# Two buffers instead of four for the rotation tables of a state-space mixer, rebuilt between the rotations

## The chip, the cores and the metric

One core of a Trainium2 chip runs the whole program, in float32. The metric is the device time of one execution in microseconds (us), the median of several. Five engines work side by side, each through its own instruction stream in order, and wait for one another on semaphores: PE (TensorE, matrix products), DVE (VectorE), ACT (ScalarE), POOL (GpSimd) and SP (here only the queue of DMA issues).

## What is computed

256 tokens of width 1024 go through three layers: a windowed-attention layer with a dense feed-forward, a forgetting-attention layer with 8 experts, and a hybrid layer (three mixers side by side) with 32 small experts. The change lies in one of the mixers of the third layer, a diagonal complex recurrence over 2048 states:

```python
mag = jnp.exp(a_re * dt)
lam_re = mag * jnp.cos(a_im * dt)
lam_im = mag * jnp.sin(a_im * dt)
...
bu_re = jnp.einsum('blgh,gph->blgp', ug, bb_re)
bu_im = jnp.einsum('blgh,gph->blgp', ug, bb_im)
_, _, h_re, h_im = lax.associative_scan(_complex_affine_combine, (lr, li, bu_re, bu_im), axis=1)
y = (jnp.einsum('blgp,ghp->blgh', h_re, c_re.astype(f32))
     - jnp.einsum('blgp,ghp->blgh', h_im, c_im.astype(f32)))
```

The output of the whole program is the normalised x after the third layer, 256 by 1024.

## The kernel before, in words

The 2048 states lie as 16 steps of 128 partitions by 256 tokens. The kernel turns the input of each state by the angle of its own decay, so that the recurrence becomes two real ones with the factor `mag`, which DVE can scan, and turns the result back. For this it needs cos and sin of 1 to 256 times the angle. They lie in four tables of 2048 columns, table q for the steps 4q to 4q+3; `s5_table(q)` says where. POOL builds a table by doubling, in `table(q, at)`: eight steps, of n = 1, 2, 4, up to 128 columns for each of four states, each of six instructions, and every one of them waits for POOL's own last result. `at` is a scratch place.

The work on step i, with q = i // 4:

- PE (`s5_steps`, the matmul helper on L704) writes two 128x256 products into the bank PB[6]; before that it waits until DVE has read those of step i-1. A step of PE later than i = 4q+4 also computes the output of the four steps of q (L1123), once POOL has turned them back.
- DVE (`turn_and_scan`, L1907 on) waits at the first step of each q for table q, then multiplies the products by the table (its helper is on L1482) and scans them (L1929, L1931).
- POOL (`turned_back`, L2720 on) waits for the scan of step i and for the output of q-1 and turns back, in six instructions (L2728 to L2735). I call this rotation i.

Where the tables lie: table 0 in GB (otherwise the gains of the norms), table 1 in the arena, table 2 at the arena's end, table 3 in Y. Y is free only after the norm "n3", which ends the expert layer. So POOL builds tables 0 to 2 early, beside the experts of the second layer (about 660 to 727 us), then does its half of the norm, builds table 3, and after that does the 16 rotations.

PE's and DVE's other work is woven in between the steps, by generators (`second_block`, `along`, `weave`): first z tiles (PE, L1140), then projections (L1093, L1102) with the first part of a recurrent mixer (`rw_first`; DVE L2010 to L2032, PE L1166), then an attention over eight heads (PE L830 scores, L842 to L846 transposes, L861 and L862; DVE L1604 mask, L1612 maxima, L1631 and L1632 normalising). The order is fixed when the program is written: an engine that waits at one step holds up all that stands behind it in its stream. In DVE's stream, step 8 stands ahead of L2019, and step 12 ahead of the mask of the third head and the normalising of the second.

The weights come by DMA into ring slots, each issued by SP when the chunk before it in the slot has been read.

Of the kernel before, what the change touches and what calls it, by code (L numbers as in the profile page):

```python
# [176 lines left out]
def drive(g):  # L177
    for _ in g:
        pass
# [22 lines left out]
def along(main, side, nm, ns):  # L202

    for k, _ in enumerate(main):
        if k % nm == nm - 1:
            for _ in range(ns):
                next(side, None)
# [23 lines left out]
def build(nc, dr, out, dbg=None):  # L231
    ctx = ExitStack()
    with ctx:
        dbg = dbg or {}

        def sb(name, n, dt=F32):
            return ctx.enter_context(nc.sbuf_tensor(name, [128, n], dt))
# [11 lines left out]
        XT = sb("XT", 8 * T)  # L249
        Y = sb("Y", 2 * D)  # L250
        GB = sb("GB", 2 * D)
        AR = sb("arena", 24080)
        SM = sb("small", 1024)
        IX = sb("ix", 64, U32)
        POS = sb("pos", T, I32)
# [9 lines left out]

        def ar(at, *shape):
            n = int(np.prod(shape))
            assert at + n <= 24080, (at, n)
            a = AR[:, at:at + n]
            if len(shape) == 2:  # L270
                return a.rearrange("p (a b) -> p a b", a=shape[0])
            if len(shape) == 3:
                return a.rearrange("p (a b c) -> p a b c", a=shape[0], b=shape[1])
            return a

        F = lambda a: a.rearrange("p a b -> p (a b)")
# [31 lines left out]
        GT = ar(3072, EARLY, 3, T)  # L308
        zT = ar(6144, 14 * 257).rearrange("p (i t) -> p i t", i=14)
        W0 = 6144 + 14 * 257  # L310
        S0 = W0 + 9728
        LW = ar(S0 + 1280, 2, 512)
        E0 = W0 + 5632
        BBt, CTt = ar(E0, 2, 512), ar(E0 + 1024, 2, 512)
        GN3 = ar(S0 + 512, 2048)
        Z = ar(10496, 2, 512)
        b5, c5 = ar(11520, 512), ar(12032, 512)
        w1, w2 = ar(12544, 16, 16), ar(12800, 16, 16)
# [24 lines left out]
        s_cum, s_ncum, s_rw1, s_rw2, s_lora, s_b5, s_c5, s_out = [  # L343
            sem("s_" + n) for n in ("cum", "ncum", "router1", "router2", "lora", "s5b", "s5c", "out")]
# [38 lines left out]
        lnM, lnP, lnD = sig("ln_gain", NORMS), sig("ln_row0", NORMS), sig("ln_row1", NORMS)  # L383
# [31 lines left out]
        tbG = sig("s5_table", range(4))  # L415
# [141 lines left out]
        for h in range(12):  # L557
            b, g = 64 * (h % 2), h // 4
# [3 lines left out]
                            v=[Vn[:, 0, g * 64:g * 64 + 64], Vn[:, 1, g * 64:g * 64 + 64]], out=mixT[:, h // 2, :]))  # L562
# [73 lines left out]

        def s5_table(q):

            t = (GB[:, :], ar(E0 + 2048, 2048), ar(S0 + 2560, 2048), Y[:, :])[q]
            return t.rearrange("p (x k t) -> p x k t", x=2, k=4)  # L640

        s5_m, s5_g = ar(S0, 2, T), ar(S0 + 512, T)
# [832 lines left out]
        def vector_program(v):  # L1475
# [111 lines left out]
            def attention(l):  # L1587
                hs, (S, PT, stat) = heads[l], abuf(l)
                n, ob = len(hs), out_banks[l]
                for i in range(n + 3):  # L1590
                    if i < n:
                        h, b = hs[i], i % 2
                        w0 = width(h)
                        wd = w0 + 256
                        sb_, st = S[i % 3], stat[:, i % 16, :]
                        v.wait_ge(*scP.at((l, i)))
                        src = PB[b]
                        if h["kind"] != "mem":
                            if i >= 3:
                                v.wait_ge(*ptP.at((l, i - 3)))  # L1600
                            if (l, i) == (2, 0):
                                v.wait_ge(*tbG.at(3))
                            if h["kind"] == "moba":
                                ins = v.scalar_tensor_tensor(sb_[:, 0:wd], c["dist"], h["slope"], src[:, 0:wd], ALU.mult, ALU.add)  # L1604
                            else:
                                ins = tt_(sb_[:, 0:wd], src[:, 0:wd], c["swa"] if h["kind"] == "swa" else c["caus"], ALU.add)
                            ins.then_inc(*DV.up(mkD, (l, i)))
                            v.wait_ge(*DV.last)
                            src = sb_
                        sink = "sink" in h  # L1610
                        v.tensor_reduce(st[:, 0:1], src[:, 0:w0], AX.X, ALU.max, negate=True).then_inc(*DV.up())
                        ins = v.tensor_reduce(st[:, 1:2], src[:, w0:wd], AX.X, ALU.max, negate=True)  # L1612
                        if sink:
                            ins.then_inc(*DV.up())
                            v.wait_ge(*DV.last)
                            v.tensor_scalar(st[:, 0:2], st[:, 0:2], nsink[:, h["sink"]:h["sink"] + 1], None, ALU.min).then_inc(*DV.up())
                            v.wait_ge(*DV.last)
                            ins = v.tensor_scalar(st[:, 4:6], st[:, 0:2], v_["sink"][:, h["sink"]:h["sink"] + 1], None, ALU.add)
                        ins.then_inc(*DV.up(mxD, (l, i)))
# [553 lines left out]
            n = 0  # L2173
# [100 lines left out]
        def scalar_program(a):  # L2274
# [197 lines left out]
            norm("n3")  # L2472
            a.wait_ge(*lnP.at("n3"))
            a.wait_ge(*lnD.at("n3"))
            a.dma_start(F(LW), dr["lora"]).then_inc(s_lora, 16)


            turned("x4")
# [202 lines left out]
        def gpsimd_program(g):  # L2681
# [57 lines left out]
            g.wait_ge(*scD_.at("cos"))  # L2739
            g.wait_ge(*scA_.at("sin"))  # L2740
            g.wait_ge(*lnD.at("n2"))
            for q in range(3):
                drive(table(q, S0))
            norm("n3")
            g.wait_ge(*lnP.at("n3"))
            g.wait_ge(*lnD.at("n3"))
            drive(table(3, W0 + 3072))
            for q in range(4):
                drive(turned_back(q))
            for st in ("n4", "n5"):  # L2750
                norm(st)

# [213 lines left out]
```

## Time and profile before

| | |
|---|---|
| three runs | 2149.57 us median, 2147.04 to 2153.64 |
| the profiled execution | 2149.57 us, span 2147.8 us |
| PE busy | 1940.7 us (90%) |
| DVE, ACT, POOL busy | 517.6, 255.9, 170.0 us |
| mean granted clock of PE | 0.956 |

The span is the time from the first to the last instruction; 1.8 us lie around it. The rows below are read like this: a start in us from the span's beginning, a duration, the engine, the line, the operation, what it writes and reads, and in brackets how long the engine had been idle before it and what ended that. The granted clock is 1.00 at PE's upper level of 2.4 GHz and 0.50 at the lower, 1.2 GHz.

The stage of the change lies between 1411 and 1608 us. In the rows `pb` is PSUM, `arena`, `GB`, `Y`, `X`, `XT`, `ringbuf` and `small` are buffers in SBUF, `cst` and `vec` constants.

### The profile page before, as it was taken

The numbers are of one execution on the slowest core, as the hardware profiler recorded it, in microseconds if no ns is written. First come the engines' busy times: TensorE is split into PE (matmuls) and PEld (weight loads), VectorE is DVE, ScalarE is ACT, GpSimd is POOL, SyncE is SP. The second block draws the span as 40 slices with busy tenths as digits, with TensorE's granted clock in tenths as the row PEclk, the third lists the DMA queues.
The fourth block names the chain that finished last, engine by engine and source line by source line (L and its number), as shares of the span: only waits on it lengthen the run. The fifth ranks groups of instructions, "written<-read, shape, count | busy, mean of one in ns | idle before, by whom it ended". The sixth has DMA issues, their size and how long they took to land.

```text
span 2147.8 us, 47628 instructions
## 1 busy us (share of the span) xinstructions
PE 1940.7 (90%) x22158; PEld 1529.0 (71%) x22158; DVE 517.6 (24%) x1204; ACT 255.9 (12%) x630; POOL 170.0 (8%) x309
## 2 busy tenths in 40 slices
PE   7998999899899999999999999977789999968764
PEld 6756885467489899999989898855457778643321
DVE  1632000222311101011100101135574332132223
ACT  1211000022111000000000000021132111010001
POOL 0000000100006400000000000054340000000000
PEclk9998999899879999999999999988899999979998
DMA  7233433321358989899898989740111045549995
GB/s 281 88 118 137 151 145 126 147 99 58 139 206 334 384 340 373 354 346 370 327 389 325 380 330 385 270 160 4 75 64 47 32 166 237 208 175 428 427 427 227
DMA packets 41009, 498.20 MB, mean 232 GB/s; under 512 B 5448, under 2 KB 5984, under 8 KB 7264
## 3 DMA queue, kind: packets, MB, share of 16 engines
q1 hardware_dynamic: 38992, 493.25, 58.1%
q8 instruction: 178, 2.92, 0.5%
q10 hardware_dynamic: 1808, 1.78, 0.3%
q14 instruction: 31, 0.25, 0.0%
HBM read 493.94 MB, written 1.05 MB: 230 GB/s over the span
## 4 chain that ended last, share of the span: by engine, by line
PE 81%; DVE 7%; DMA 7%; issue 2%; ACT 2%; DVEq 0%; SPq 0%
PE pb L1001 22%; PE pb L1020 11%; PE pb L695 11%; PE pb L704 6%; PE pb L700 5%; DMA ringbuf<-in_e2in 4%; PE pb L768 4%; PE pb L903 4%; DVE arena L1482 2%; PE pb L1152 2%; PE pb L1417 2%; PE pb L944 2%; PE pb L1140 2%; PE pb L830 1%; PE pb L789 1%
## 5 line engine op out<-in xcount | busy, mean ns | idle before, releaser
L1001 PE MATMUL pb<-arena,ringbuf 128*64 128x80 f32 (+1 forms) x9856 | 481.5, 240 | 5.9 <-issue 5.7
L1001 PEld LDWEIGHTS pb<-arena,ringbuf 128*64 128x64 f32 (+1 forms) x9856 | 464.5, 145 | 25.8 <-issue 11.5
L1020 PE MATMUL pb<-arena,ringbuf 128*64 128x80 f32 (+1 forms) x4928 | 232.5, 239 | 6.2 <-issue 6.2
L1020 PEld LDWEIGHTS pb<-arena,ringbuf 128*64 128x64 f32 (+1 forms) x4928 | 228.3, 145 | 10.1 <-issue 7.8
L1482 DVE TENSOR_TENSOR arena<-arena,pb 128x160 f32<-128x160 f32 (+3 forms) x154 | 58.1, 377 | 716.5 <-ACT arena L2459 438.3
L695 PE MATMUL pb<-XT,ringbuf 128*128 128x256 f32 (+1 forms) x976 | 217.9, 385 | 3.0 <-ACT XT L2276 1.9
L695 PEld LDWEIGHTS pb<-XT,ringbuf 128*128 128x128 f32 (+1 forms) x976 | 186.8, 192 | 32.1 <-issue 3.2
L2276 ACT ACTIVATE arena<-pb 128x256 f32<-128x256 f32 (+4 forms) x163 | 68.2, 436 | 474.3 <-PE pb L1020 114.0
L704 PE MATMUL pb<-arena 64*64 64x64 f32 (+4 forms) x664 | 107.5, 325 | 15.4 <-ACT ringbuf L2557 4.4
L704 PEld LDWEIGHTS pb<-arena 64*64 64x64 f32 (+4 forms) x664 | 52.4, 154 | 68.0 <-issue 38.5
L2684 POOL TENSOR_TENSOR X<-Y,GB 128x1024 f32<-128x1024 f32 x5 | 11.7, 2340 | 1106.6 <-DVE Y L1482 1106.6
L2459 ACT ACTIVATE arena<-pb 128x160 f32<-128x160 f32 x88 | 26.8, 304 | 585.4 <-PE pb L1001 585.4
L768 PE MATMUL pb<-XT,ringbuf 128*128 128x256 f32 x400 | 95.2, 390 | 0.9 <-ACT XT L2276 0.9
L700 PE MATMUL pb<-ringbuf,arena 128*128 128x512 f32 x192 | 85.1, 604 | 2.8 <-DVE arena L1482 1.8
L768 PEld LDWEIGHTS pb<-XT,ringbuf 128*128 128x128 f32 x400 | 75.2, 194 | 16.4 <-issue 5.7
L903 PE MATMUL pb<-ringbuf,arena 128*128 128x512 f32 x176 | 75.7, 592 | 0.0
L700 PEld LDWEIGHTS pb<-ringbuf,arena 128*128 128x128 f32 x192 | 37.0, 194 | 49.5 <-issue 47.3
L726 PE MATMUL pb<-cst,X 128*128 128x128 f32 x96 | 23.2, 423 | 51.8 <-POOL X L2684 41.8
L903 PEld LDWEIGHTS pb<-ringbuf,arena 128*128 128x128 f32 x176 | 33.4, 190 | 41.7 <-issue 41.4
L1449 PE MATMUL pb<-ringbuf,arena 128*32 128x512 f32 x272 | 38.7, 693 | 24.2 <-DMA ringbuf<-in_e2in 24.2
L726 PEld LDWEIGHTS pb<-cst,X 128*128 128x128 f32 x96 | 18.9, 223 | 58.3 <-POOL X L2684 45.9
L944 PEld LDWEIGHTS pb<-arena,X 128*64 128x64 f32 (+1 forms) x768 | 52.5, 167 | 10.1 <-DVE arena L1482 4.8
(349 smaller groups left out, 1909.1 us busy)
## 6 DMA issues: line engine op xcount, KB each, us to landing
ringbuf<-in_ein SPq DMA_DIRECT2D x88, 2048.0 KB, 10.3
ringbuf<-in_eout SPq DMA_DIRECT2D x64, 1408.0 KB, 7.6
ringbuf<-in_e2in SPq DMA_DIRECT2D x17, 2048.0 KB, 30.6
arena<-in_e2in SPq DMA_DIRECT2D x15, 2048.0 KB, 27.0
ringbuf<-in_fin SPq DMA_DIRECT2D x11, 2048.0 KB, 7.7
ringbuf<-in_e2out SPq DMA_DIRECT2D x10, 2048.0 KB, 23.3
ringbuf<-in_wo SPq DMA_DIRECT2D x6, 2048.0 KB, 7.9
ringbuf<-in_gate SPq DMA_DIRECT2D x8, 1536.0 KB, 7.5
```

Source lines behind the costliest of these rows:

```text
L695: ins = pe.matmul(outp, w[:, j, col:col + m], rT[:, j, :], start=j == 0, stop=j == kt - 1)
L700: ins = pe.matmul(outp, aT[:, j, tt * 128:(tt + 1) * 128], w[:, j, col:col + n], start=j == 0, stop=j == kt - 1)
L704: return pe.matmul(o, l, r, start=True, stop=True)
L768: ins = pe.matmul(PB[b][:, i * 256:i * 256 + 256], held["p"][:, j, (col0 + i) * 128:(col0 + i + 1) * 128], xT[:, j, :], start=j == 0, stop ...
L903: ins = pe.matmul(PB[2 * h + tt][:, :], hT[:, f + j, tt * 128:(tt + 1) * 128], w3[:, j, h * 512:(h + 1) * 512], start=f + j == 0, stop=f + ...
L944: ins = pe.matmul(PB[b][h_, k * n:(k + 1) * n], x3[:, tt, dt_ * 128 + h_.start:dt_ * 128 + h_.stop], PS_[i][:, tt, :], start=tt == 0, stop ...
L1001: ins = pe.matmul(PB[b][h_, t * C1:(t + 1) * C1], w3[:, k, t * 128 + h_.start:t * 128 + h_.stop], XG[e % 2][:, k, :], start=k == 0, stop=k ...
L1020: ins = pe.matmul(PB[d // 4][h_, (d % 4) * C1:(d % 4 + 1) * C1], w3[:, f, h_], HT[:, f, :], start=f == 0, stop=f == 21)
L1140: ins = pe.matmul(z_bank(k)[:, 0:256], w3[:, j, o:o + 128], xT[:, j, :], start=j == 0, stop=j == 7)
L1152: ins = pe.matmul(PB[5][:, 0:256], w3[:, j, br * 128:(br + 1) * 128], xT[:, j, :], start=j == 0, stop=j == 7)
L1482: return v.tensor_tensor(o, a, b, op)
L2276: return a.activation(dst, src, ACT.Copy, scale=1.0 if scale is None else scale)
```

## The change

Two places hold the four tables: GB those of even q, the arena's place of table 1 those of odd q. Tables 0 and 1 are built early as before. Tables 2 and 3 are built between POOL's rotations: `along(turned_back(1), table(2, ...), 1, 2)` runs one rotation, then two of the eight doubling steps, and so on. Table 2 is so written into GB after rotations 4 to 7, and table 3 over table 1 after rotations 8 to 11. DVE's separate wait for table 3 ahead of the attention goes, the arena becomes 580 columns shorter, and some places in it are moved.

```diff
-        AR = sb("arena", 24080)
+        AR = sb("arena", 23500)
...
-        S0 = W0 + 9728
-        LW = ar(S0 + 1280, 2, 512)
+        S0 = W0 + 10496
+        LW = ar(S0 + 2048, 2, 512)
...
-        GN3 = ar(S0 + 512, 2048)
+        GN3 = ar(S0 + 1024, 2048)
...
-            t = (GB[:, :], ar(E0 + 2048, 2048), ar(S0 + 2560, 2048), Y[:, :])[q]
+            t = GB[:, :] if q % 2 == 0 else ar(E0 + 2048, 2048)
...
-                            if (l, i) == (2, 0):
-                                v.wait_ge(*tbG.at(3))
...
-            a.dma_start(F(LW), dr["lora"]).then_inc(s_lora, 16)
+            a.dma_start(ar(S0 + 2048, 1024), dr["lora"]).then_inc(s_lora, 16)
...
-            for q in range(3):
-                drive(table(q, S0))
+            drive(table(0, S0))
+            drive(table(1, S0))
             norm("n3")
-            g.wait_ge(*lnP.at("n3"))
-            g.wait_ge(*lnD.at("n3"))
-            drive(table(3, W0 + 3072))
-            for q in range(4):
-                drive(turned_back(q))
+            drive(turned_back(0))
+            along(turned_back(1), table(2, S0 + 1280), 1, 2)
+            along(turned_back(2), table(3, S0 + 1280), 1, 2)
+            drive(turned_back(3))
```

POOL's stream around the norm "n3" before: the last instruction of table 2, the norm, the first of table 3. `ln_gain`, `ln_row1` and `ln_row0` are the norm's semaphores, `s5_table` and `pool_own` those of the tables and of POOL itself.

```order
L2696 TENSOR_TENSOR arena<-arena 128x512
L2715 TENSOR_TENSOR arena<-arena 128x4x128 [waits pool_own]
L2684 TENSOR_TENSOR X<-Y,arena 128x1024 [waits ln_gain,s5_table]
L2702 COPY Y<-small 128x4 [waits ln_row1,ln_row0]
L2703 COPY Y<-small 128x4
```

And now, two lines up in the file: the last of table 1, the norm, and the first rotation.

```order
L2694 TENSOR_TENSOR arena<-arena 128x512
L2713 TENSOR_TENSOR arena<-arena 128x4x128 [waits pool_own]
L2682 TENSOR_TENSOR X<-Y,arena 128x1024 [waits ln_gain,s5_table]
L2726 TENSOR_TENSOR arena<-arena,GB 128x256 [waits s5_scan]
L2727 TENSOR_TENSOR arena<-arena,GB 128x256
```

One table of 50 instructions has gone from ahead of the norm, and one from behind it. POOL's stream between rotation 7 and rotation 8 before: nothing stands there (`s5_y` is PE's output of a q, `s5_scan` DVE's scan, `s5_back` POOL's rotation).

```order
L2733 TENSOR_TENSOR arena<-arena 128x256
L2735 TENSOR_TENSOR arena<-arena 128x256 [waits pool_own]
L2728 TENSOR_TENSOR arena<-arena 128x256 [waits s5_y,s5_scan,s5_back]
L2729 TENSOR_TENSOR arena<-arena 128x256
L2731 TENSOR_TENSOR arena<-arena 128x256 [waits pool_own]
```

And now, between these two rotations:

```order
L2693 TENSOR_TENSOR GB<-GB 128x4x64 [waits s5_back]
L2694 TENSOR_TENSOR arena<-GB 128x4x64
L2710 TENSOR_TENSOR GB<-GB,arena 128x4x64 [waits pool_own]
L2693 TENSOR_TENSOR GB<-GB 128x4x64 [waits pool_own]
L2694 TENSOR_TENSOR arena<-GB 128x4x64
L2713 TENSOR_TENSOR GB<-GB,arena 128x4x64 [waits pool_own]
L2693 TENSOR_TENSOR GB<-GB 128x4x128 [waits pool_own]
L2694 TENSOR_TENSOR arena<-GB 128x512
L2710 TENSOR_TENSOR GB<-GB,arena 128x4x128 [waits pool_own]
L2693 TENSOR_TENSOR GB<-GB 128x4x128 [waits pool_own]
L2694 TENSOR_TENSOR arena<-GB 128x512
L2713 TENSOR_TENSOR GB<-GB,arena 128x4x128 [waits pool_own]
```

These are the two largest doubling steps of table 2; rotation 8 follows. Between rotations 11 and 12 stand those of table 3 in the same way. DVE's stream at step 8 keeps its order and its waits; before:

```order
L1482 TENSOR_TENSOR ringbuf<-ringbuf 128x512 [waits rw1_act,dve_own]
L1482 TENSOR_TENSOR arena<-pb,arena 128x512 [waits rw1_dve,s5_in,s5_table]
L1482 TENSOR_TENSOR arena<-arena 128x256 [waits s5_back,dve_own]
L1482 TENSOR_TENSOR arena<-pb,arena 128x256 [waits dve_own]
L1482 TENSOR_TENSOR arena<-pb,arena 128x256
L1482 TENSOR_TENSOR arena<-arena 128x256 [waits s5_in_read]
```

And now the table is read from GB, and `s5_table` is waited for in the same place:

```order
L1482 TENSOR_TENSOR ringbuf<-ringbuf 128x512 [waits rw1_act,dve_own]
L1482 TENSOR_TENSOR arena<-pb,GB 128x512 [waits rw1_dve,s5_in,s5_table]
L1482 TENSOR_TENSOR arena<-arena 128x256 [waits s5_back,dve_own]
L1482 TENSOR_TENSOR arena<-pb,GB 128x256 [waits dve_own]
L1482 TENSOR_TENSOR arena<-pb,GB 128x256
L1482 TENSOR_TENSOR arena<-arena 128x256 [waits s5_in_read]
```

## Rows read from the trace of the kernel before

**Rows 1.** The page: busy time of each engine.

```profile
PE 1940.7 (90%) x22158; PEld 1529.0 (71%) x22158; DVE 517.6 (24%) x1204; ACT 255.9 (12%) x630; POOL 170.0 (8%) x309
```

**Rows 2.** Timeline of PE: start, us, engine, line, op, out<-in, count [idle before <-releaser].

```profile
1409.48 1.97 PE L726 MATMUL pb<-cst,X 128*128 128x128 f32 x8 [14.82 <-POOL X L2684]
...
1513.07 1.13 PE L1093 MATMUL pb<-XT,ringbuf 128*128 128x256 f32 x4
1520.69 1.12 PE L1166 MATMUL pb<-cst,ringbuf 128*128 128x128 f32 x4 [6.49 <-DVE ringbuf L2019]
...
1569.54 1.13 PE L1140 MATMUL pb<-XT,ringbuf 128*128 128x256 f32 x4
1571.95 0.33 PE L842 MATMUL pb<-cst,arena 128*128 128x128 f32 x1 [1.28 <-DVE arena L1632]
```

**Rows 3.** Timeline of DVE, the two table changes and the steps behind them.

```profile
1515.66 0.69 DVE L1482 TENSOR_TENSOR arena<-pb,arena 128x512 f32<-128x512 f32 x1
...
1519.95 0.68 DVE L2019 SCALAR_TENSOR_TENSOR ringbuf<-ringbuf 128x512 f32<-128x512 f32 x1
...
1532.54 0.94 DVE L1931 TENSOR_TENSOR_SCAN arena<-small,arena 128x256 f32<-128x256 f32 x1
...
1557.04 0.69 DVE L1931 TENSOR_TENSOR_SCAN arena<-small,arena 128x256 f32<-128x256 f32 x1
...
1565.75 0.69 DVE L1482 TENSOR_TENSOR arena<-pb,Y 128x512 f32<-128x512 f32 x1 [1.18 <-PE pb L704]
...
1571.54 0.35 DVE L1632 TENSOR_SCALAR arena<-arena,small 128x256 f32<-128x256 f32 x1
```

**Rows 4.** Timeline of POOL: one table, first instructions of its steps, and its last.

```profile
1411.90 0.19 POOL L2702 COPY Y<-small 128x4 f32<-128x4 f32 x1 [2.47 <-DVE X L1482]
...
1415.28 0.21 POOL L2695 TENSOR_TENSOR Y<-Y 128x16 f32<-128x16 f32 x1
...
1418.52 0.29 POOL L2695 TENSOR_TENSOR Y<-Y 128x64 f32<-128x64 f32 x1
...
1423.21 0.61 POOL L2695 TENSOR_TENSOR Y<-Y 128x256 f32<-128x256 f32 x1
...
1432.61 1.09 POOL L2715 TENSOR_TENSOR Y<-Y,arena 128x512 f32<-128x512 f32 x1
```

**Rows 5.** Timeline of POOL: ends and starts of rotations 6, 7, 10 and 11.

```profile
1498.27 0.73 POOL L2735 TENSOR_TENSOR arena<-arena 128x256 f32<-128x256 f32 x1
1510.61 0.64 POOL L2728 TENSOR_TENSOR arena<-arena 128x256 f32<-128x256 f32 x1 [11.61 <-issue]
...
1515.05 1.05 POOL L2735 TENSOR_TENSOR arena<-arena 128x256 f32<-128x256 f32 x1
...
1552.19 0.72 POOL L2735 TENSOR_TENSOR arena<-arena 128x256 f32<-128x256 f32 x1
1557.86 0.64 POOL L2728 TENSOR_TENSOR arena<-arena 128x256 f32<-128x256 f32 x1 [4.94 <-issue]
...
1561.34 0.72 POOL L2735 TENSOR_TENSOR arena<-arena 128x256 f32<-128x256 f32 x1
```

**Rows 6.** Windows: from:to and length, busy us of each engine, PE's granted clock, DMA.

```profile
core 0: us, PE busy (x) PEld busy (x) DVE busy (x) ACT busy (x) POOL busy (x), PEclk, DMA share, GB/s
1412.00:1416.00 4.00, 3.00 (x11) 2.45 (x12) 1.36 (x6) 1.20 (x2) 3.18 (x17) 0.50 0.42 133
1416.00:1420.00 4.00, 4.00 (x15) 3.32 (x15) 0.00 (x0) 0.00 (x0) 3.33 (x14) 0.73 0.00 0
1522.00:1524.00 2.00, 2.00 (x6) 1.62 (x5) 0.70 (x2) 0.44 (x1) 0.00 (x0) 0.51 0.00 0
705.00:727.00 22.00, 20.67 (x349) 17.57 (x348) 3.77 (x8) 1.50 (x4) 19.50 (x49) 1.00 1.00 414
1566.00:1603.00 37.00, 33.49 (x168) 22.04 (x167) 35.58 (x84) 11.86 (x39) 18.14 (x24) 1.00 0.12 43
```

**Rows 7.** Issues on SP's queue: the first expert weights of the last stage.

```profile
1756.53 1.56 SPq L2820 DMA_DIRECT2D arena<-in_e2in  x3
```

**Rows 8.** The expert weights' tensor: who waited for its transfers, us, times.

```profile
  PE pb L1449: 37.1, 17
```

More of the change, by code:

```diff
@@ L267, in ar @@
             n = int(np.prod(shape))
-            assert at + n <= 24080, (at, n)
+            assert at + n <= 23500, (at, n)
             a = AR[:, at:at + n]
```

## The prediction, written before the run

> **What bounds the kernel now.** I first read the page's busy times: PE works 1940.7 us of a span of 2147.8, the others a quarter of it or less [rows 1]. So a change on POOL, which is busy 170.0 us, can cost or bring something only where PE waits. Next come the waits of PE in the stage from 1411 to 1608 us, then the timelines of DVE and POOL beside them, because both tables that are moved are made by POOL and read by DVE. Three things are to be seen there.
>
> PE is not saturated in this stage, and where it waits it waits mostly for DVE. Ahead of L1166 at 1520.69 it was idle 6.49 us for DVE's L2019 (the work of 1513.07 ends at 1514.20), and ahead of L842 at 1571.95 it was idle 1.28 us for L1632 [rows 2]. DVE, for its part, goes without a gap from step 8 at 1515.66 to L2019 at 1519.95, and reaches step 12 at 1565.75 and L1632 at 1571.54 [rows 3]. From 1566 to 1603 it is busy 35.58 of 37 us [rows 6]: what makes it late there stays.
>
> POOL, in the same stage, has long idle times ahead of its rotations (11.61 us ahead of rotation 7, 4.94 ahead of rotation 11 [rows 5]). These are where the change means its tables to be built. The question is how much of a table falls into such an idle time and how much into the time when DVE already needs it.
>
> **What one table costs.** Table 3 is the pattern [rows 4]. It starts at 1411.90 and its last instruction ends at 1432.61 + 1.09 = 1433.70, 21.8 us. Split as the change splits it, two doubling steps at a time: copies and the first two steps to 1415.28, 3.38 us; the next two to 1418.52, 3.24; the next two to 1423.21, 4.69; the last two to 1433.70, 10.49. Half of a table lies in the last pair, and the last pair stands behind the last rotation of the q.
>
> **What is removed.** Table 2 goes from about 705 to 727 us. There PE is busy 20.67 of 22 us at full clock beside it [rows 6], so at most 1.33 us can come back, and nothing shows that POOL made them; I take 0. Table 3 goes from 1412 to 1434. Between 1412 and 1416 PE is busy 3.00 of 4 us, and in the next four all the time [rows 6]; it waits for the turned x, not for POOL. At most 1.0, I take 0. The separate wait of DVE for table 3 ahead of the attention: table 3 was ready at 1433.70 and DVE comes to the attention only behind step 11, whose scan ends at 1557.73 [rows 3], so 0. The moved places in the arena and the shorter arena change no instruction's size: 0. All of these together bring 0, at most 2.3 us.
>
> **What table 2 adds.** Rotation 4 is followed by 3.38 us and rotation 5 by 3.24 us of table; rotation 6 ends at 1498.27 + 0.73 = 1499.00 and is followed by 4.69, to 1503.7. Rotation 7 started at 1510.61 [rows 5]. So three of the four pairs are hidden in POOL's idle time, with 6.9 us to spare, and rotation 7 still ends at 1515.05 + 1.05 = 1516.10. Then comes the last pair: 1516.10 + 10.49 = 1526.6. DVE wants the table at 1515.66 [rows 3]. It is held for 1526.6 - 1515.7 = 10.9 us, and with it everything queued behind step 8: L1949, L2019 and the rest of the recurrent mixer's first part. L2019 would start at 1530.9 and PE's L1166 at 1531.6 instead of 1520.69. PE has nothing it may do meanwhile: it stands at L1166 in its own stream since 1514.20. ACT waits for PE or DVE, POOL's rotation 8 for PE's output of q = 1, which is behind L1166. Nothing in the stage runs on, so I take the whole 10.9 us. The bounds: POOL's last pair has no competition while DVE stands still, as table 3 had none, so the duration can hardly differ; rotation 7 itself overlaps the same DVE work as before. 10.4 to 11.5.
>
> **What table 3 adds.** Times are in the frame of before; all are later by 10.9. Rotation 8 and 9 with their pairs end well before rotation 10. Rotation 10 ends at 1552.91, its pair 4.69 later at 1557.60, and rotation 11 started at 1557.86 [rows 5], so it is only just hidden. Here DVE works at the same time (step 11, whose scan ends at 1557.04 + 0.69 [rows 3]). When the two run together both take longer: the scan at 1532.54, beside rotation 8, took 0.94 us against 0.69 for the one at 1557.04, which ran without POOL [rows 3], and the last instruction of rotation 7 took 1.05 against 0.72 for rotation 11's [rows 5]. By such ratios the 4.69 us, for the greater part beside DVE, can become 5.5, and step 11 on DVE longer by some 0.8: rotation 11 starts 0 to 1.0 us later; I take 0.7. It ended at 1561.34 + 0.72 = 1562.06; with the last pair, 1562.06 + 0.7 + 10.49 = 1573.25. DVE wants table 3 for step 12 at 1565.75: 7.5 us of waiting, 6.8 at least, 8.3 at most.
>
> The Trainium skill, "SBUF — State Buffer", section "SBUF: two separate sides", says that VectorE and GpSimd share a port pair as an exclusive lock, and that a VectorE operation with two SBUF inputs and a GpSimd operation that reads SBUF block each other for a whole instruction. By that rule the overlap at step 11 is a matter of which engine starts first, and a scan or a product could be late by a whole instruction of the other. The rows above agree in kind, and the sum does not use the rule.
>
> Is this wait on the path? What stands behind step 12 in DVE's stream is the mask of the third head and the normalising of the second; PE's L842 at 1571.95 waited for the latter already and was idle 1.28 us [rows 2]. So PE is later by all 7.5. Afterwards DVE is busy 35.58 of 37 us [rows 6] and PE 33.49: DVE can regain 1.4 us at most, and I take none of it. Behind the stage everything follows from this work.
>
> **What the clock adds.** After an idle time PE gets the lower level for a while. After the 6.49 us it still had 0.51 from 1522 to 1524 [rows 6]; after the 14.82 us ahead of 1409.48 it had 0.50 from 1412 to 1416 and 0.73 in the four after [rows 2, 6]. The first idle time now becomes 17.4 us and the second 8.8 us instead of 1.28. Half clock costs half of the work done under it: 3.3 us of it are there after the first wait already; with the stretch of the longer idle time (about 8.8 us from 1409.48 to the rise at about 1418) there would be 5.5 more, 2.7 us lost. After the second idle time, new, 3 to 8 us at half clock lose 1.5 to 4 us of PE, of which part is hidden under DVE, which is fuller. Together 0 to 5; the near row is the one after 6.49 us, since the rise there is 3 to 4 us after the start. I take 1.0.
>
> **Sum.** 10.9 + 7.5 + 1.0 - 0 = 19.4 us. The profiled execution took 2149.57 us (span 2147.8 and 1.8 around it), which is the median of the three runs. 2149.6 + 19.4 = 2169.0 us, 0.9% slower. Its own range: least 10.4 + 6.8 - 1.4 - 1.0 = 14.8, most 11.5 + 8.3 + 5 = 24.8, so 2164 to 2174.
>
> **The rivals.**
>
> *Only the first wait counts.* Between L842 and the end of the stage PE and DVE both have work for one another, eight heads deep; if DVE's later work were less tied to step 12 than I read, PE could work ahead and the 7.5 us would vanish for the most part. For it: PE's idle time at 1571.95 is only 1.28 us, and PE holds 3.5 us of free time between 1566 and 1603. Against it: DVE itself is full, and a full engine does not catch up. Time: 2149.6 + 10.9 + 1 = 2161.5. Chance 0.12.
>
> *The clock costs its full price.* Both idle times fall so that PE works at 1.2 GHz as long as after 1409.48, without cover: 10.9 + 7.5 + 5 and up to 1 more from contention, 2174. For it are the rows of 1412 to 1420. Against it: the waits after the second idle time are DVE's. Chance 0.14.
>
> *The last stage takes the delay in.* At the end PE waits 37.1 us, 17 times, for the expert weights [rows 8]. If those transfers ran on while POOL holds the others up, PE would find them landed, and up to all 19.4 us would be absorbed: 2149.6, not slower. It decides from the point at which the transfers are issued. Against it: the first three are issued at 1756.53 [rows 7], long behind both waits and behind work that is late with them, so they are late by as much. Chance 0.03 for no change, and 0.02 for faster, if the removed 2.3 us should count as well (2147).
>
> *The change does what it says:* the order of POOL's stream shows the last pair behind rotations 7 and 11, so I see no case in which the tables come earlier.
>
> The forecast keeps 0.69. About 0.3% (6.4 us) is what a measurement of this kernel can tell from no change. The forecast and the first two rivals are slower by more: 0.95. Same 0.03, faster 0.02. The range for 8 in 10 takes in the forecast's own 2164 to 2174, the first rival's 2161.5 and most of the second, with the spread of the runs: 2160 to 2176.
>
> **What the profile would show.** DVE's first product of step 8 has an idle time of about 11 us ahead of it, ended by POOL's L2713, and that of step 12 about 8, ended by the same. PE's L1166 of step 8 has about 17.4 us ahead of it instead of 6.49, and the first L842 of the second head about 8.8 instead of 1.28. POOL builds table 2 in four pieces, the first three before rotation 7 without making it late. All that comes after 1608 is as long as before, PE's 37 us on the weights too. I am wrong if rotation 11 is late by several us (then the second wait is longer), if DVE shows gaps between 1580 and 1620 that let the second wait go, or if PE's granted clock is lower over more than a few us after the waits.

## The result and the profile after

Four runs of the changed kernel had a median of 2174.7 us (2166.5 to 2178.3), against 2150.1 for the kernel before: a ratio of 1.0108, with an interval of 1.0076 to 1.0142. Beside the later experiments it was measured again: 2171.4 us, 1.0117 (1.0090 to 1.0144). By these ratios the change costs 23 to 25 us. The prediction was 19.4 us, a time of 2169.0 in a range of 2160 to 2176.

The profiled execution took 2172.19 us, with a span of 2170.4 and a mean granted clock of 0.947 (0.956 before).

POOL's timeline in the changed kernel: the end of rotation 7 and of table 2, the end of the third pair of table 3, the start of rotation 11 and the end of table 3; answers to [rows 5]:

```profile
1512.25 1.05 POOL L2733 TENSOR_TENSOR arena<-arena 128x256 f32<-128x256 f32 x1
...
1522.75 1.09 POOL L2713 TENSOR_TENSOR GB<-GB,arena 128x512 f32<-128x512 f32 x1
...
1566.69 0.46 POOL L2713 TENSOR_TENSOR arena<-arena 128x128 f32<-128x128 f32 x1
1567.23 0.79 POOL L2726 TENSOR_TENSOR arena<-arena,GB 128x256 f32<-128x256 f32 x1
...
1581.52 1.26 POOL L2713 TENSOR_TENSOR arena<-arena 128x512 f32<-128x512 f32 x1
```

Rotation 7 ends at 1512.25 + 1.05 = 1513.30, and the last pair of table 2 follows only then and ends at 1522.75 + 1.09 = 1523.84. So too for table 3: its third pair ends at 1567.15, rotation 11 follows at once (it had 4.94 us to spare before), and the last pair ends at 1582.78.

DVE's timeline at step 8, at the scan of step 11, at step 12 and at step 13; answers to [rows 3]:

```profile
1523.88 0.69 DVE L1482 TENSOR_TENSOR arena<-pb,GB 128x512 f32<-128x512 f32 x1 [11.16 <-POOL GB L2713]
...
1564.72 0.94 DVE L1927 TENSOR_TENSOR_SCAN arena<-small,arena 128x256 f32<-128x256 f32 x1
...
1582.81 0.69 DVE L1482 TENSOR_TENSOR arena<-pb,arena 128x512 f32<-128x512 f32 x1 [7.62 <-POOL arena L2713]
...
1593.66 0.69 DVE L1482 TENSOR_TENSOR arena<-pb,arena 128x512 f32<-128x512 f32 x1 [2.08 <-PE pb L704]
```

DVE stands idle 11.16 and 7.62 us, both times until POOL's last instruction of a table, L2713. Before, no wait of DVE ended at POOL here.

PE's timeline; answers to [rows 2]. The rows of L704 with 32*128 are the products of steps 8, 12 and 14:

```profile
1402.29 1.97 PE L726 MATMUL pb<-cst,X 128*128 128x128 f32 x8 [15.10 <-POOL X L2682]
...
1509.20 1.13 PE L704 MATMUL pb<-arena 32*128 32x256 f32 x4
...
1528.90 1.12 PE L1166 MATMUL pb<-cst,ringbuf 128*128 128x128 f32 x4 [17.51 <-DVE ringbuf L2017]
...
1568.52 2.84 PE L1140 MATMUL pb<-XT,ringbuf 128*128 128x256 f32 x8 [2.73 <-ACT arena L2274]
...
1576.46 1.13 PE L704 MATMUL pb<-arena 32*128 32x256 f32 x4
...
1581.47 1.13 PE L1140 MATMUL pb<-XT,ringbuf 128*128 128x256 f32 x4
1589.01 0.47 PE L842 MATMUL pb<-cst,arena 128*128 128x128 f32 x1 [6.42 <-DVE arena L1630]
...
1603.86 1.13 PE L704 MATMUL pb<-arena 32*128 32x256 f32 x4
...
1626.76 1.07 PE L1123 MATMUL pb<-arena 128*32 128x256 f32 x16
```

L1166 was idle 17.51 us instead of 6.49, as predicted (17.4). L842 was idle 6.42 instead of 1.28; 8.8 was predicted. The reason is to be seen at 1568.52: PE was idle 2.73 us there and then took 2.84 us for eight products, and 3.67 for the next eight, and so it handed over step 12 late itself. In the kernel before, the same wait was 2.27 us and the products behind it took 1.96:

```profile
1559.86 1.96 PE L1140 MATMUL pb<-XT,ringbuf 128*128 128x256 f32 x8 [2.27 <-ACT arena L2276]
```

PE's clock in the changed kernel, in windows (columns as in [rows 6]):

```profile
core 0: us, PE busy (x) PEld busy (x) DVE busy (x) ACT busy (x) POOL busy (x), PEclk, DMA share, GB/s
1529.00:1531.00 2.00, 2.00 (x7) 1.82 (x8) 1.88 (x4) 0.60 (x1) 0.00 (x0) 0.50 0.00 0
1570.00:1576.00 6.00, 6.00 (x15) 3.99 (x14) 2.16 (x6) 0.99 (x4) 5.53 (x10) 0.50 0.00 1
1576.00:1578.00 2.00, 2.00 (x9) 1.15 (x8) 0.00 (x0) 0.89 (x2) 1.96 (x2) 0.93 0.00 0
1590.00:1596.00 6.00, 6.00 (x26) 2.87 (x26) 3.75 (x12) 2.14 (x7) 0.31 (x1) 0.50 0.00 0
```

Behind the first wait the clock is at the lower level, 0.50, as it was before the change [rows 6]. From 1570 to 1576 PE is busy all the time and has the lower level too, and again from 1590 to 1596, behind the second wait. Before, the clock was 1.00 from 1566 to 1603 [rows 6].

A second profile of the same kernel tells what is fixed in this and what is chance. PE's timeline in it, the same places:

```profile
1398.28 1.97 PE L726 MATMUL pb<-cst,X 128*128 128x128 f32 x8 [15.09 <-POOL X L2682]
...
1500.64 1.13 PE L704 MATMUL pb<-arena 32*128 32x256 f32 x4
...
1520.34 1.12 PE L1166 MATMUL pb<-cst,ringbuf 128*128 128x128 f32 x4 [17.52 <-DVE ringbuf L2017]
...
1566.63 1.13 PE L704 MATMUL pb<-arena 32*128 32x256 f32 x4
...
1580.90 0.47 PE L842 MATMUL pb<-cst,arena 128*128 128x128 f32 x1 [8.13 <-DVE arena L1630]
...
1598.48 1.13 PE L704 MATMUL pb<-arena 32*128 32x256 f32 x4
...
1621.39 1.07 PE L1123 MATMUL pb<-arena 128*32 128x256 f32 x16
```

And steps 8, 12 and 14 and the last output in the kernel before:

```profile
1512.01 1.13 PE L704 MATMUL pb<-arena 32*128 32x256 f32 x4
...
1564.53 1.13 PE L704 MATMUL pb<-arena 32*128 32x256 f32 x4
...
1583.22 1.13 PE L704 MATMUL pb<-arena 32*128 32x256 f32 x4
...
1607.39 1.07 PE L1123 MATMUL pb<-arena 128*32 128x256 f32 x16
```

Distances from the first product behind the norm (L726, the rows at 1409.48, 1402.29 and 1398.28), in us:

| PE reaches | before | after | again | more than before |
|---|---|---|---|---|
| step 8 (L704) | 102.5 | 106.9 | 102.4 | 4.4 / -0.2 |
| L1166, behind the first wait | 111.2 | 126.6 | 122.1 | 15.4 / 10.9 |
| step 12 (L704) | 155.1 | 174.2 | 168.4 | 19.1 / 13.3 |
| L842, behind the second wait | 162.5 | 186.7 | 182.6 | 24.3 / 20.2 |
| step 14 (L704) | 173.7 | 201.6 | 200.2 | 27.8 / 26.5 |
| last output (L1123) | 197.9 | 224.5 | 223.1 | 26.6 / 25.2 |

The first wait adds 11.0 us in both. The second adds 5.1 and 6.9. What is left of 26.6 and 25.2 us is 4.4 / -0.2 ahead of the first wait, 3.7 / 2.4 between the two and 3.5 / 6.3 behind the second, less the 1.2 or 1.3 that DVE and PE regain at the end. These are nearly all stretches of half clock: taken over windows of 1 us from the first product to the last output, PE's busy time times what the clock lacked of 1.00 is 12.3 and 8.2 us more than before, where the three pieces sum to 11.6 and 8.5. The little that remains includes short waits that grew, as the one of 2.73.

The stage alone does not make the difference of two profiles. Up to the first product behind the norm the changed kernel was 7.2 us ahead of the kernel before in the first profile and 11.2 us in the second; behind the last output it was 3.2 us slower and 1.3 us faster. So the second profiled execution took only 2162.3 us, the least of its six runs. The start of the stage differs by chance: in nine profiles of kernels that are alike up to there it lies between 1398.3 and 1412.0 us (1409.5 before the change).

### The profile page after: what moved, and what is told of

It is laid out like the page before. It is cut to its first block, busy times and chain, and to the rows that moved or that the text cites. A ratio compares the mean times of both kernels' runs of the same rounds, so it can differ in the third digit from the quotient of the medians.

```text
span 2170.4 us, 47625 instructions
## 1 busy us (share of the span) xinstructions
PE 1947.6 (90%) x22158; PEld 1535.2 (71%) x22158; DVE 517.4 (24%) x1204; ACT 255.8 (12%) x630; POOL 171.0 (8%) x309
## 3 DMA queue, kind: packets, MB, share of 16 engines
HBM read 493.94 MB, written 1.05 MB: 228 GB/s over the span
## 4 chain that ended last, share of the span: by engine, by line
PE 80%; DMA 7%; DVE 6%; issue 2%; POOL 2%; ACT 2%; DVEq 0%; SPq 0%; POOLq 0%
PE pb L1001 22%; PE pb L1020 11%; PE pb L695 11%; PE pb L704 6%; PE pb L700 4%; DMA ringbuf<-in_e2in 4%; PE pb L768 4%; PE pb L903 3%; PE pb L1152 2%; DVE arena L1482 2%; PE pb L1417 2%; PE pb L1140 2%; PE pb L944 2%; PE pb L830 1%; PE pb L789 1%
## 5 line engine op out<-in xcount | busy, mean ns | idle before, releaser
L704 PE MATMUL pb<-arena 64*64 64x64 f32 (+4 forms) x664 | 111.0, 333 | 15.0 <-DVE Y L1482 3.5
L704 PEld LDWEIGHTS pb<-arena 64*64 64x64 f32 (+4 forms) x664 | 54.3, 158 | 68.7 <-issue 38.2
L768 PE MATMUL pb<-XT,ringbuf 128*128 128x256 f32 x400 | 96.1, 393 | 0.9 <-ACT XT L2274 0.9
L726 PE MATMUL pb<-cst,X 128*128 128x128 f32 x96 | 23.4, 427 | 52.3 <-POOL X L2682 42.0
L1140 PE MATMUL pb<-XT,ringbuf 128*128 128x256 f32 x224 | 57.8, 405 | 3.2 <-ACT arena L2274 3.2
L726 PEld LDWEIGHTS pb<-cst,X 128*128 128x128 f32 x96 | 19.0, 224 | 58.7 <-POOL X L2682 46.2
```

The costliest lines, as they stand in the source:

```text
L704: return pe.matmul(o, l, r, start=True, stop=True)
L768: ins = pe.matmul(PB[b][:, i * 256:i * 256 + 256], held["p"][:, j, (col0 + i) * 128:(col0 + i + 1) * 128], xT[:, j, :], start=j == 0, stop ...
L1140: ins = pe.matmul(z_bank(k)[:, 0:256], w3[:, j, o:o + 128], xT[:, j, :], start=j == 0, stop=j == 7)
```

## The experiments

Each was measured beside the kernel before, on the same chip. The medians come from four groups of runs, in which the kernel before had 2147.2 to 2150.9 us, so kernels are compared by the ratio.

| kernel | median us | ratio | interval |
|---|---|---|---|
| three_steps | 2156.8 | 1.0024 | 1.0011 to 1.0038 |
| only_table2_late | 2169.5 | 1.0093 | 1.0072 to 1.0114 |
| only_table3_late | 2165.1 | 1.0069 | 1.0047 to 1.0091 |
| pe_kept_busy | 2173.3 | 1.0100 | 1.0072 to 1.0128 |
| pe_busy_fit | 2163.9 | 1.0062 | 1.0040 to 1.0083 |
| last_pair_twice | 2185.0 | 1.0174 | 1.0150 to 1.0198 |
| steps_3_4_1 | 2159.5 | 1.0044 | 1.0023 to 1.0064 |
| before_pe_filled | 2141.5 | 0.9957 | 0.9932 to 0.9981 |
| three_steps_pe_filled | 2153.4 | 1.0023 | 1.0007 to 1.0039 |
| table_extra_early | 2174.9 | 1.0126 | 1.0099 to 1.0153 |
| changed_again | 2171.4 | 1.0117 | 1.0090 to 1.0144 |
| table3_in_y_pe_filled | 2145.3 | 0.9988 | 0.9968 to 1.0008 |

**three_steps: the same tables, earlier in POOL's stream.** Edit of the changed kernel:

```diff
-            along(turned_back(1), table(2, S0 + 1280), 1, 2)
-            along(turned_back(2), table(3, S0 + 1280), 1, 2)
+            along(turned_back(1), table(2, S0 + 1280), 1, 3)
+            along(turned_back(2), table(3, S0 + 1280), 1, 3)
```

> The changed kernel with three doubling steps behind each rotation instead of two, for tables 2 and 3, so that the last two steps stand behind rotations 6 and 10 and nothing of a table behind rotations 7 and 11. Theory (the time is what DVE waits for the two tables, with what PE's lower clock costs after it): table 2 is ready before rotation 7 starts, table 3 at about 10.5 us after rotation 10 ends, which is 2 us before DVE wants it; both idle times of DVE ended by POOL are gone, PE waits about 6.5 us at L1166 as before the change, time 2147 to 2154, as the kernel before. Rival (the cost is POOL work beside DVE in this stage, or the moved places, whatever the order): the table work in the stage is the same, so most of the 23 us stays, 2165 to 2175.

With one number in each line changed both waits at POOL are gone from the profile, and with them some 18 to 20 of the 23 to 25 us. The rival (POOL's work in this stage costs the time wherever it stands) falls for the greater part. But 0.24% stay, where the theory had none (2156.8 us, and at most 2154 was expected), and PE's wait at L1166 is 7.9 us, not 6.5.

**only_table2_late and only_table3_late: one wait each.** The edit above for one of the two lines.

> Three steps behind each rotation for table 3 only; table 2 as in the changed kernel, so only the first wait stays. Theory: DVE waits 11 us for table 2 and none for table 3; 11 us and 1 to 3 for the clock, 2161 to 2165. Rival, the sum is not of two separate waits but the clock's: about half of 23 us or less, with no idle time of DVE to show for it.

> Three steps behind each rotation for table 2 only; only the second wait stays. In the profile of the changed kernel PE came to step 12 late by 3.3 us at half clock, so the wait for table 3 cost only 5.1 us there. Theory: now the wait is 6.9 to 8.3 us if PE is not slowed ahead of step 12, time 2156 to 2161. Rival (PE and DVE regain it in the attention): 2150 to 2153.

DVE's idle times are as expected, 11.2 us for table 2 in the one and 7.6 for table 3 in the other, and both were slower by more than expected, 20 and 15 us over before (0.93% and 0.69% of 2150) instead of 11 to 15 and 6 to 11. If the 5 us that three_steps keeps are in both, which is not shown, the two waits are 15 and 10 us above it, at the upper end of what was expected. The second wait is not covered, since 1.0069 lies clear of 1.0024. By these numbers both together should be 30 us over before and are 23 to 25; each ratio is uncertain by 3 to 5 us, so this is near the edge of what can be told, and I conclude nothing from it.

**last_pair_twice: a longer wait.** `table` makes the steps n = 64 and n = 128 of table 2 a second time before it signals.

```diff
-            along(turned_back(1), table(2, S0 + 1280), 1, 2)
+            along(turned_back(1), table(2, S0 + 1280, 1), 1, 2)    # the last pair once more
```

> The changed kernel, with the last two doubling steps of table 2 made twice ahead of the signal. DVE's wait for table 2 grows by 10.5 us to 21.7. Theory that nothing runs on while DVE waits: the time rises by 10 to 12 us over the changed kernel, 2184 to 2187. Rival, that part of a longer wait is covered by other work: less than 8 us more.

DVE's waits in it, in us, times, longest:

```profile
DVE arena L1482 <- POOL GB L2714: 21.7, 1, 21.7
...
DVE arena L1482 <- POOL arena L2714: 7.6, 1, 7.6
```

10.5 us more of waiting, and a ratio of 1.0174 beside 1.0108 and 1.0117: 12 to 14 us by the ratios, 10 to 14 by the medians. So nothing runs on while DVE waits for table 2.

**pe_kept_busy and pe_busy_fit: what the lower clock costs.** Products that nobody reads, ahead of PE's two waits:

```diff
+                if j == 0:
+                    for _ in range(28):                  # pe_busy_fit: 18
+                        one(PB[3][:, :], ident, CST[:, 0:512])
                 pe.wait_ge(*dv("at"))
...
+                        if (l, k) == (2, 1):
+                            for _ in range(12):          # pe_busy_fit: 7
+                                one(PB[3][:, :], ident, CST[:, 0:512])
                         pe.wait_ge(*nmD.at((l, k)))
```

> The changed kernel with 28 more products of 128x512 on PE ahead of its wait for the first held work, and 12 ahead of its wait in the attention (their results are not used). They fill the idle time and end before it. Theory that the lower clock after the idle times costs several us: the granted clock stays 1.00 through both waits and the 8 us behind them, the two waits stay 11 and 5 to 8 us, and the time falls by 3 to 7 us, to 2167 to 2172. Theory that only the waits cost: no change, 2174. If the products last longer than the wait, the time rises.

I had taken one such product for half of what it lasts (28 took 24.0 us, 0.86 each), and the products ended 6.4 and 2.0 us after DVE's work was there. The expected fall did not come (2173.3 us, six runs from 2165.2 to 2183.8). Nor did the time rise above that of the changed kernel, so the products gave back about what they added.

> The run before with the idle times filled had too many products: 28 lasted 24.0 us for a wait of 17.5, 12 lasted 10.3 for 8.8, so some 7 us were added and the time still did not rise. Now 18 (15.4 us by that measure) and 7 (6.0 us). Theory that PE's lower clock after the two idle times costs several us of the change: 2173 minus 4 to 8, so 2166 to 2170, with DVE's waits unchanged at 11.2 and 7.6 us. Theory that it costs 1 us or less, as the prediction had it: 2173 to 2175.

PE's timeline in pe_busy_fit, and then windows around the two waits (columns as in [rows 6]):

```profile
1517.15 15.61 PE L704 MATMUL pb<-cst 128*128 128x512 f32 x36
1534.82 0.66 PE L1171 MATMUL pb<-cst,ringbuf 128*128 128x128 f32 x4 [2.06 <-DVE ringbuf L2023]
...
1584.10 6.17 PE L704 MATMUL pb<-cst 128*128 128x512 f32 x14
1592.36 0.33 PE L847 MATMUL pb<-cst,arena 128*128 128x128 f32 x1 [2.09 <-DVE arena L1636]
```

```profile
1512.00:1548.00 36.00, 29.29 (x111) 16.91 (x109) 19.83 (x32) 4.30 (x10) 20.54 (x25) 1.00 0.00 0
1580.00:1600.00 20.00, 17.91 (x82) 10.58 (x82) 13.29 (x31) 3.12 (x11) 9.78 (x11) 1.00 0.00 1
```

The products end 2 us before PE is released, DVE's waits are 11.2 and 7.6 us as ever, and the clock is 1.00 through both places. Behind the wait of L1145 between them (2.69 us, L1140 in the other kernels), which was not filled, eight products still took 3.58 us. The ratio falls from 1.0108 / 1.0117 to 1.0062: 10 to 12 us, more than expected (2163.9 us instead of 2166 to 2170), and as much as the first wait. A part of it was there before the change already, as the next run shows.

**before_pe_filled: the same in the kernel before.** 4 products ahead of the turned x (`fill(4)`, where PE was idle 14.8 us), and 3, 1, 3, 6 and 3 ahead of five waits in `rw_first(0)`.

```diff
+            def fill(n):
+                for _ in range(n):
+                    one(PB[3][:, :], ident, CST[:, 0:512])
...
+            fill(4)                       # ahead of the turned x
...
+                fill(0 if j else 6)       # ahead of the wait on "at"; likewise 3, 1, 3 and 3 at four others
```

> The kernel before the change, with PE's idle times of this stage filled with products whose results are not used: 4 ahead of the turned x, then 3, 1, 3, 6 and 3 ahead of the waits of 3.4, 1.8, 4.4, 6.5 and 4.4 us in the recurrent mixer's first part. Theory that half clock after short idle times costs in this kernel too: 22 us stand at 0.5 between 1477 and 1543, about half of them with PE at work, so 3 to 6 us less, 2145 to 2148. Rival, that the added products cost as much as they give: 2149 to 2153.

Windows from 1470 to 1545 (columns as in [rows 6]), first of the kernel before, then of this one:

```profile
1470.00:1545.00 75.00, 53.20 (x206) 36.31 (x204) 38.30 (x59) 11.95 (x25) 26.93 (x36) 0.82 0.14 53
```

```profile
1470.00:1545.00 75.00, 65.80 (x250) 39.58 (x248) 42.25 (x67) 13.35 (x28) 30.80 (x42) 0.98 0.15 56
```

The clock rises from 0.82 to 0.98, and the kernel is 0.43% faster (interval 0.9932 to 0.9981), by more than expected (2141.5 us instead of 2145 to 2148). It is the fastest of all here. By distances as in the table above it gains 6.7 us up to step 11 (136.6 instead of 143.4) and keeps them.

**three_steps_pe_filled, steps_3_4_1 and table3_in_y_pe_filled: the rest of three_steps.**

steps_3_4_1 splits the eight steps of a table as 3, 4, 1 (three_steps: 3, 3, 2), so that only the last stands between rotations 6 and 7, and 10 and 11; three_steps_pe_filled is three_steps with the products of before_pe_filled.

```diff
-            along(turned_back(1), table(2, S0 + 1280), 1, 2)
-            along(turned_back(2), table(3, S0 + 1280), 1, 2)
+            for q, at in ((1, 2), (2, 3)):
+                steps = table(at, S0 + 1280)
+                for k, _ in enumerate(turned_back(q)):
+                    for _ in range((3, 4, 1, 0)[k]):
+                        next(steps, None)
```

> Doubling steps of tables 2 and 3 behind the rotations as 3, 4, 1 and 0. With three steps each (3, 3, 2) no wait for a table was left, but 5 us more than before the change, and the wait at L1166 was 7.9 instead of 6.5 us. Theory that the rest is POOL and DVE holding each other up where they overlap (steps 6, 7 and 10, 11 of DVE beside the two largest doublings): less overlap there, 2 to 4 us less than 2157, 2152 to 2155. Rival, it is the granted clock by chance: 2155 to 2158.

> Two buffers with three doubling steps behind each rotation, and the same 20 products in PE's idle times that made the kernel before faster by 0.43%. What is left between the two is then not the lower clock of these places. Theory that POOL's table work in the stage costs some 3 to 5 us by holding DVE up (the wait of L1140 at ACT's copy was 4.2 us instead of 2.7, that of L1166 7.9 instead of 6.5): 2145 to 2147, against 2141.5. Rival, that the rest of three_steps (0.24%) was the granted clock: 2141 to 2143.

Both came out slower than either theory had it. Another split of the eight steps brought nothing (1.0044, 2159.5 us; at most 2158 was expected), and with the filling, which gave the kernel before 9 us, the two-buffer kernel stayed at 1.0023 (2153.4 us; at most 2147). So 0.66%, 14 us, lie between the two filled kernels. The profile of three_steps_pe_filled keeps pace with that of before_pe_filled to within 3 us up to step 11; at step 12 it is 9.2 us behind, and at the last output 14.1. Here is DVE at step 11 and PE behind it in three_steps; the edit puts the largest doubling of table 3 beside them:

```profile
1558.90 1.21 DVE L1927 TENSOR_TENSOR_SCAN arena<-small,arena 128x256 f32<-128x256 f32 x1
1560.14 1.03 DVE L1929 TENSOR_TENSOR_SCAN arena<-small,arena 128x256 f32<-128x256 f32 x1
```

```profile
1563.57 3.75 PE L1140 MATMUL pb<-XT,ringbuf 128*128 128x256 f32 x8 [3.71 <-ACT arena L2274]
```

The scans took 0.68 and 0.69 us where POOL stood still. PE waits 3.71 us instead of 2.27 (it waits for ACT's copy, which stands behind a tanh that waits for DVE), and the eight products behind take 3.75 us instead of 1.96, which are the numbers of before at 1559.86. Behind the same wait, in three_steps_pe_filled and in before_pe_filled:

```profile
1550.85 3.75 PE L1145 MATMUL pb<-XT,ringbuf 128*128 128x256 f32 x8 [4.15 <-ACT arena L2284]
```

```profile
1550.97 1.97 PE L1145 MATMUL pb<-XT,ringbuf 128*128 128x256 f32 x8 [2.27 <-ACT arena L2286]
```

1.9 us more of idle time, and the granted clock is 0.50 from 1551 to 1560, where it stayed at its upper level in before_pe_filled. In table3_in_y_pe_filled table 3 was therefore put back into Y and made behind the norm, as before the change; table 2 has the split of steps_3_4_1, and the products stay:

```diff
-            t = GB[:, :] if q % 2 == 0 else ar(E0 + 2048, 2048)
+            t = (GB[:, :], ar(E0 + 2048, 2048), GB[:, :], Y[:, :])[q]
...
+            drive(table(3, S0 + 1280))
             drive(turned_back(0))
```

> With both tables rebuilt in time and PE's idle times filled, 0.66% stay between the two-buffer kernel and the kernel before with the same filling. In the profile they open at DVE's step 11, which runs beside the largest doubling of table 3: its scans take 1.21 and 1.03 us instead of 0.68 and 0.69, PE's wait at L1145 behind it is 4.2 instead of 2.3 us, and PE then works about 10 us at half clock. Here table 3 goes back to Y and to the place after the norm, and table 2 alone is rebuilt, into GB, with 3, 4, 1 and 0 steps behind the rotations. Theory that table 3 beside step 11 is the cause: the scans take 0.7 us, the wait is 2.3 and the clock stays 1.00, 2141 to 2145. Rival, that reading GB or the moved places or table 2's overlap is the cause: 2149 to 2154.

DVE's scans of step 11 in this kernel, and PE's wait behind them:

```profile
1542.77 0.68 DVE L1937 TENSOR_TENSOR_SCAN arena<-small,arena 128x256 f32<-128x256 f32 x1
1543.49 0.69 DVE L1939 TENSOR_TENSOR_SCAN arena<-small,arena 128x256 f32<-128x256 f32 x1
```

```profile
1546.40 3.43 PE L1145 MATMUL pb<-XT,ringbuf 128*128 128x256 f32 x8 [2.36 <-ACT arena L2284]
```

The scans take 0.68 and 0.69 us and the wait is 2.36, as the theory has it, but the clock was low behind this wait all the same (3.43 us for the eight products). The ratio, 0.9988, lies below that of three_steps_pe_filled and above that of before_pe_filled, and its interval touches both. That POOL beside step 11 lengthens DVE's scans and PE's wait is shown.

In this profile table 2's overlap has a part as well. Its last step now stands beside DVE's step 7, whose scans take 1.54 and 1.40 us instead of 0.69, and PE's wait behind them is 3.70 us. First this kernel, then before_pe_filled:

```profile
1493.48 1.54 DVE L1937 TENSOR_TENSOR_SCAN arena<-small,arena 128x256 f32<-128x256 f32 x1
...
1506.66 1.12 PE L1171 MATMUL pb<-cst,ringbuf 128*128 128x128 f32 x4 [3.70 <-DVE ringbuf L2027]
```

```profile
1504.63 0.69 DVE L1939 TENSOR_TENSOR_SCAN arena<-small,arena 128x256 f32<-128x256 f32 x1
...
1516.25 0.66 PE L1171 MATMUL pb<-cst,ringbuf 128*128 128x128 f32 x4 [1.33 <-DVE ringbuf L2029]
```

The granted clock of this kernel is 0.50 from 1506 to 1512. It was 0.2 us behind before_pe_filled at step 8, is 5.5 us behind at step 9, and 9.2 at the last output. In three_steps_pe_filled the scans of step 7 took 1.54 and 1.40 us too and PE's wait was 2.90, but the clock stayed at its upper level and only 1.5 us were lost there. How the 0.24% are shared between the two tables, as a mean over many runs, stays open.

**table_extra_early: POOL's early work.** Table 0 is made twice, so that POOL works as long beside the experts as before the change.

```diff
+            drive(table(0, S0, True))     # True: without the table's signal
             drive(table(0, S0))
```

> The changed kernel, with table 0 made once more early, so that POOL works as long beside the experts as in the kernel before (three tables). The prediction took the removal of the third early table as worth 0, at most 1.3 us. Theory: the same as the changed kernel, 2172 to 2176. Rival, that POOL's early work slows the experts, whose stage was 7 us shorter in the profile of the changed kernel: 3 to 7 us more, 2177 to 2181.

1.0126 (2174.9 us, as the theory had it) beside 1.0117 for changed_again, measured beside it: no difference that these intervals (0.27% to either side) can tell, so a few us stay possible. Its stage starts at 1401.6 us, with three early tables; with two it started at 1402.3 and 1398.3. So nothing shows that the third early table made the expert layer longer before the change.

> The changed kernel once more, beside the other two on the same chip: 2172 to 2176 by its own runs, and a second profile, to see which of its costs are the same in both: both theories expect waits of 11.2 and 5 to 7.6 us, and the sum of the two with the clock's 7 to 9 us to make the whole difference. In which places the clock is low differs from run to run.

DVE's waits were 11.2 and 7.6 us, as expected, and the median of 2171.4 us lies 0.6 below what was expected. Its profile stands above.

## Why the prediction was right, and where not

The direction, the range and the mechanism of the two waits held; the forecast of 2169.0 was 2 to 6 us low (2171.4 and 2174.7). The time lies at least as near to that of the second rival, the full price of the clock (2174, chance 0.14), and the runs bear out a good part of that rival. One of the signs of being wrong that were named did come: the granted clock was low over more than a few us behind the waits. That the time still fell into the range is in part luck: the clock cost more than the 5 us that were its bound, while the second wait cost PE less than forecast and 1.2 us of it came back.

*The table's length and its split.* 10.49 us for the last pair were taken from table 3 of before. In the changed kernel they were 10.5 (1513.38 to 1523.84) and 11.0 (1571.75 to 1582.78). Right but for 0.5 us. DVE stood idle beside most of the second, so it is not what made it longer: POOL's last additions of 128x512 take 1.26 us there and 1.09 in table 2. In the kernel before, too, they took 1.27 us in the tables that lay in the arena with their scratch place, and 1.09 in GB and Y. Table 3 was moved from Y into the arena. Rotation 11 started 0.7 us late (5.7 us behind the end of rotation 10 instead of 4.9), as forecast.

*The first wait.* 10.9 us forecast, 11.0 on PE's path in both profiles. That nothing runs on meanwhile was argued in the prediction; last_pair_twice shows it.

*The second wait.* 7.5 us forecast at DVE, 7.6 measured in every kernel that has it. On PE's path it was 5.1 and 6.9, since PE came late by itself at half clock. The rival that only the first wait counts fell: only_table3_late is slower by 0.69%. PE and DVE regained 1.2 or 1.3 us of it, where 1.4 was the bound and none was taken.

*What is removed, at 0.* Nothing speaks against it: table_extra_early tells no difference, and the first six steps start within 1 us of before, counted from the first product behind the norm.

*The clock, at 1.0 us.* This is the term that was mis-sized. Its bound was 0 to 5, and the value was taken from the nearer row, the short wait of before. The table above has 7 and 9 us behind the first wait (3.7 + 3.5 and 2.4 + 6.3), nearly all of it half clock, and pe_busy_fit gives back 10 to 12 (of which a part was lost before the change too, as before_pe_filled shows). Two things were not seen. Half clock was costed only behind the two new waits; but a part of it came behind an old wait, at L1140, that grew to 2.73 and 2.69 us in the two profiles (2.27 before): there the eight products behind it had the upper level before (1.96 us) and the lower one now, while POOL's third pair lengthened DVE's scan of step 11 (0.94 us instead of 0.68). The prediction had this overlap, and DVE later by 0.8 us in it, but counted it only as a delay of rotation 11, not as a longer wait of PE. And behind the second wait I had hidden a part of PE's loss under DVE; but PE's slow products are what DVE waits for there (2.08 us at step 13), so they came through.

The rule of the Trainium skill that was weighed, in "SBUF — State Buffer", section "SBUF: two separate sides", lets a VectorE operation with two SBUF inputs and a GpSimd operation that reads SBUF block each other for a whole instruction. The scans beside POOL's work took 1.21 and 1.03 us in three_steps instead of 0.68 and 0.69, which agrees in kind; the rows do not tell a lock from slower sharing.

## What to carry to other kernels

A buffer that is reused costs nothing only if its refill ends before the reader comes, and even then 0.24% stayed here, and the refill was seen to slow its neighbour. Put the long steps of the refill into the helper's idle times, and not behind the last reader. Here the largest two of eight steps were half of the work, and moving them forward by one place took back four fifths of the loss. Cost a wait of PE as its length and what follows at half clock, and look also at the short waits that it or a busier neighbour makes a little longer.

## What was not expected of the hardware

PE's clock is worth more than the waits suggest: 20 products without use, 16 of them in idle times of 2 to 6 us and 4 in one of 15, made the kernel before faster by 0.43%, with the mean granted clock going from 0.82 to 0.98 over 75 us. The products behind the wait of L1140 kept the upper level after 2.27 us of idle time and lost it after 2.36 in another kernel. One and the same wait of 3.40 us in the recurrent mixer, which the change does not touch, had four products of 1.10 us behind it in the profile before and in the second one of the changed kernel, and of 2.04 us in the first. So runs of one kernel differ too: 23 runs of the kernel before went from 2138.9 us at a mean clock of 0.957 to 2161.0 at 0.953. A few us of a profile that is taken once are not a property of the kernel.
